# A hybrid decoder block on one core: the last sixteen tiles made of high and low halves

## The chip, the cores and the metric

The kernel runs on one core of a Trainium2 chip, written engine by engine in Bass: TensorE (PE), VectorE (DVE), ScalarE (ACT), GpSimd (POOL) and the sync engine (SP) each have their own list of instructions, and semaphores order them. The metric is the device time of one execution in microseconds, the median of several runs.

## The reference, cut to what matters

One decoder block on 272 tokens (16 meta tokens and 256) of width 1024, all in float32. The steps that the change touches are these:

```python
u = rms_norm(h, norm1_w)
proj = einsum('bld,dn->bln', u, w_in)          # 9232 columns: q,k,v | q,k,v | gate | beta, decay | gA | gB
y_a = differential_attention(...)              # 8 heads of 128
y_d = gated_deltanet(...)                      # chunked delta rule, 8 heads of 128
y_a = einsum('ble,ed->bld', y_a, w_branch_attn)
y_d = einsum('ble,ed->bld', y_d, w_branch_dn)
mixed = sigmoid(gate_a) * y_a + sigmoid(gate_d) * y_d
h = h + einsum('bld,de->ble', mixed, w_out)
h = h + hierarchical_moe(rms_norm(h, norm2_w), ...)   # 32 experts of width 256, top 2 in one of 4 groups
return rms_norm(h, final_norm_w)[:, 16:]
```

## The kernel before, in words

The products with `w_in`, `w_branch_attn`, `w_branch_dn` and `w_out` are cut into 96 tiles (`TILES`), eight of each kind, in the order ak, av, aq, dq, dk, dv, gate, ga, ya, gb, yd, out. Two tiles share a unit of 1 MB of weights; the sync engine loads units into a ring of six slots (L458), and slots 6 to 11 of the same ring hold buffers until the experts' weights come. A tile of ak to yd is the product of 128 weight columns with all tokens, 8 steps deep; TensorE's `tile(n)` writes it to bank n % 2.

Most tiles are made of halves: `split_high` (ScalarE, L278) rounds the 128x1024 weights of a tile to float32r (`w_hi`), `split_low` (VectorE, L283) subtracts that from the weights (`w_lo`), and TensorE takes hi x hi, hi x lo and lo x hi (L740), 24 matmuls of the program a tile. `SPLIT` lists these tiles, all but ya and out; `AHEAD = 3` says how many tiles ahead a split is made, and `NSPLIT = AHEAD + 2` how many pairs of buffers there are, in slots 6 to 10. The other operand is split once: `uT_hi`/`uT_lo` for the tokens, `yd_hi`/`yd_lo` for the delta rule's result. The ya tiles (L722, operand `yaT`) and the out tiles (L729, operands `mixT` and the ring's unit) are plain float32 products, 8 matmuls of the program each.

The order is written out by hand. Tiles up to dq go one after another. Then come 26 turns (`SLOTS_A`), in each of which TensorE does one tile (dq0 to gate1) and a part of the attention and of the convolution's sums, and VectorE one part of softmax, of the convolution (L1578) and of the gating (L1591), then the split (`split_lows`). The delta rule follows (`MIX_ORDER` for TensorE, `BEHIND` for the others): ten steps for the meta tokens, then 18 steps (s0 to s7, x1, t1, x2, t2, x3, t3, w, v, o, q) for each half of the tokens, each in two chains of four heads, with a tile between steps: ya0 before t3, ya1 before v, ya2 before o, ya3 after q of the first half and before s0 of the second, ya4 before s2, ya5 before s3, ya6 before s5, ya7 before s6. In `BEHIND` a split stands where its tile stands in `MIX_ORDER`, and the tile's evacuation (`tile_out`) behind the next step. GpSimd does one product in s1, s7, t1 and q (L651, L657).

Then gb4 to gb7, yd0 to yd7 and out0 to out7 run on TensorE back to back. For yd VectorE multiplies with the gate (L1652) and adds both branches into `mixT` (L1653, semaphore `mixed`); out0 waits for all of them. An out tile is one of the two halves of the tokens by 256 columns; VectorE adds it to `h_tok` (L1658). From out2 on TensorE turns the finished columns (`piece_turn`, L1003), and `piece_logits` (L1012) makes the router's logits of them; its first call waits for six small loads (`norms_in`) that ScalarE issues behind its last split (L1384 to L1389). The routing and eight batches of four experts end the kernel: gather (L1057), gate and up (L1069), down (L1088), back (L1095). The sync engine prefetches expert units as slots come free (`wait_tiles`), then 12 units for each batch, released by `gu_used` and `down_used`.

## Time and profile before

| | us |
|---|---|
| median of 3 runs | 745.88 (745.85 to 747.65) |
| the profiled execution | 743.06 |
| its span | 741.3 |
| TensorE busy | 628.2 (85%) |
| weight loads busy | 498.3 (67%) |
| VectorE busy | 322.0 (43%) |
| ScalarE busy | 247.1 (33%) |
| GpSimd busy | 46.1 (6%) |

The page cuts the span into 40 slices of 18.5 us; each digit is a busy share in tenths, PEclk the granted clock of TensorE in tenths of full speed:

```profile
PE   2899999899999979999898999976896686867954
DVE  4534349899878647522634273143210110201103
ACT  5335547667674434313222550121110110101102
PEclk9989999999999989999999999997999988978988
GB/s 292 252 137 167 157 153 114 105 70 112 114 114 132 153 57 59 59 57 57 52 132 104 2 260 262 423 255 1 346 422 422 422 422 422 422 422 423 421 385 57
```

Counted from 1, slices 7 to 13 are the attention turns, 14 to 23 the delta rule, 24 to 27 yd and out, and the experts begin in slice 28. Busy times are those of engines, which work beside each other, so they don't add up to the span; a busy share says nothing of what ends last.

### The profile page before, as it was taken

To read this page: it belongs to the slowest core of one execution; us is meant where nothing else is said; L and a number is where in the kernel's file an instruction comes from. 1 tells how busy PE (TensorE), PEld (TensorE's weight loads), DVE (VectorE), ACT (ScalarE), POOL (GpSimd) and SP (SyncE) were. 2 spreads that over 40 slices of the span, in tenths; PEclk is the share of its full clock that TensorE was granted. 3 is DMA by queue.
4 is the path that set the end of the run, shared out by engine and by line. 5 is a ranking of instruction groups with operands and counts; after the bars stand their busy time and mean duration, and the time that the engine had idled before them with its cause. 6 is when DMAs were issued, how large, how long until landed. Compare 5 with 4: busy or idle time off the path is not lost.

```text
span 741.3 us, 12849 instructions
## 1 busy us (share of the span) xinstructions
PE 628.2 (85%) x5127; PEld 498.3 (67%) x5127; DVE 322.0 (43%) x717; ACT 247.1 (33%) x548; POOL 46.1 (6%) x94
## 2 busy tenths in 40 slices
PE   2899999899999979999898999976896686867954
PEld 2899998789988879987788898854333323413321
DVE  4534349899878647522634273143210110201103
ACT  5335547667674434313222550121110110101102
POOL 8000000000000001201111100020000000000000
PEclk9989999999999989999999999997999988978988
DMA  9845443323334411111143077960899999999991
GB/s 292 252 137 167 157 153 114 105 70 112 114 114 132 153 57 59 59 57 57 52 132 104 2 260 262 423 255 1 346 422 422 422 422 422 422 422 423 421 385 57
DMA packets 69686, 156.40 MB, mean 211 GB/s; under 512 B 7042, under 2 KB 56308, under 8 KB 57348
## 3 DMA queue, kind: packets, MB, share of 16 engines
q1 hardware_dynamic: 65792, 154.36, 55.5%
q10 hardware_dynamic: 3844, 1.34, 0.7%
q8 instruction: 35, 0.57, 0.3%
q14 instruction: 15, 0.12, 0.0%
HBM read 154.64 MB, written 1.05 MB: 210 GB/s over the span
## 4 chain that ended last, share of the span: by engine, by line
PE 67%; DMA 16%; DVE 7%; ACT 4%; issue 3%; SPq 1%; POOL 1%; DVEq 0%; ACTq 0%; POOLq 0%
PE bank L740 29%; DMA arena<-in_expert_w_up_dram 15%; PE bank L1069 9%; PE bank L909 4%; PE bank L722 4%; PE bank L729 4%; PE bank L887 2%; PE bank L851 1%; PE bank L828 1%; PE bank L1088 1%; PE bank L1057 1%; SPq L481 1%; PE bank L1095 1%; PE bank L796 1%; DVE w_lo L283 1%
## 5 line engine op out<-in xcount | busy, mean ns | idle before, releaser
L740 PE MATMUL bank<-uT_hi,w_hi 128*128 128x272 f32 (+1 forms) x576 | 175.7, 305 | 5.7 <-issue 4.2
L740 PE MATMUL bank<-uT_lo,w_hi 128*128 128x272 f32 (+1 forms) x576 | 166.7, 289 | 0.0
L740 PE MATMUL bank<-uT_hi,w_lo 128*128 128x272 f32 (+1 forms) x576 | 166.5, 289 | 0.0
L283 DVE TENSOR_TENSOR w_lo<-arena,w_hi 128x1024 fp32r<-128x1024 f32 x80 | 98.6, 1235 | 48.3 <-ACT w_hi L278 48.0
L740 PEld LDWEIGHTS bank<-uT_hi,w_hi 128*128 128x128 f32 x576 | 111.4, 193 | 8.5 <-issue 6.8
L740 PEld LDWEIGHTS bank<-uT_lo,w_hi 128*128 128x128 f32 x576 | 111.5, 194 | 1.5 <-issue 0.5
L740 PEld LDWEIGHTS bank<-uT_hi,w_lo 128*128 128x128 f32 x576 | 111.3, 193 | 0.0
L1069 PE MATMUL bank<-arena 128*32 128x512 f32 x512 | 68.8, 698 | 42.3 <-DMA arena<-in_expert_w_up_dram 39.1
L278 ACT ACTIVATE w_hi<-arena 128x1024 fp32r<-128x1024 f32 x80 | 83.8, 1052 | 4.5 <-PE bank L740 4.2
L1069 PEld LDWEIGHTS bank<-arena 128*32 128x32 f32 x512 | 19.7, 126 | 85.7 <-issue 85.7
L1875 DVE COPY arena<-bank 128x256 f32<-128x256 f32 x8 | 3.4, 425 | 108.6 <-PE bank L1076 108.6
L1423 ACT ACTIVATE arena<-bank 128x256 f32<-128x256 f32 x8 | 3.1, 384 | 120.9 <-PE bank L1069 120.9
L1578 DVE SCALAR_TENSOR_TENSOR arena<-arena 128x272 f32<-128x272 f32 x72 | 37.8, 525 | 7.5 <-ACT arena L1210 5.8
L1088 PE MATMUL bank<-arena 128*32 128x512 f32 x256 | 34.0, 679 | 4.1 <-DVE arena L1882 4.1
L909 PE MATMUL bank<-arena 64*64 64x64 f32 x964 | 34.2, 220 | 1.5 <-ACT arena L1346 0.8
L909 PEld LDWEIGHTS bank<-arena 64*64 64x64 f32 x964 | 31.1, 134 | 5.8 <-issue 1.5
L1057 PEld LDWEIGHTS bank<-arena 128*128 128x128 f32 x256 | 31.1, 199 | 3.3 <-issue 3.3
L1057 PE MATMUL bank<-arena 128*128 128x128 f32 x256 | 31.2, 282 | 0.0
L1095 PE MATMUL bank<-arena 128*128 128x512 f32 x64 | 29.6, 605 | 0.0
L729 PE MATMUL bank<-arena 128*128 128x256 f32 x128 | 28.7, 380 | 1.1 <-DVE arena L1653 1.1
L722 PE MATMUL bank<-arena 128*128 128x256 f32 x128 | 29.3, 382 | 0.0
L729 PEld LDWEIGHTS bank<-arena 128*128 128x128 f32 x128 | 24.0, 190 | 4.3 <-issue 1.2
(319 smaller groups left out, 867.6 us busy)
## 6 DMA issues: line engine op xcount, KB each, us to landing
arena<-in_w_in_dram SPq DMA_DIRECT2D x36, 1024.0 KB, 5.2
arena<-in_expert_w_gate_dram SPq DMA_DIRECT2D x32, 1024.0 KB, 16.7
arena<-in_expert_w_up_dram SPq DMA_DIRECT2D x32, 1024.0 KB, 18.5
arena<-in_expert_w_down_dram SPq DMA_DIRECT2D x32, 1024.0 KB, 17.6
arena<-in_w_branch_attn_dram SPq DMA_DIRECT2D x4, 1024.0 KB, 5.0
arena<-in_w_branch_dn_dram SPq DMA_DIRECT2D x4, 1024.0 KB, 5.2
arena<-in_w_out_dram SPq DMA_DIRECT2D x4, 1024.0 KB, 5.1
arena<-in_x_dram SPq DMA_DIRECT2D x4, 512.0 KB, 5.0
```

What stands on the lines that cost most here:

```text
L278: nc.scalar.activation(w_hi[q % NSPLIT], split_source(nc.scalar, q), ACT.Copy).then_inc(w_hi_ready, 1)
L283: nc.vector.tensor_tensor(w_lo[q % NSPLIT], src, w_hi[q % NSPLIT].bitcast(F32), ALU.subtract).then_inc(w_lo_ready, 1)
L722: last = pe.matmul(ps[:, 0:SEQ], unit(u)[:, c, half * P:(half + 1) * P], yaT[:, c, :], start=(c == 0), stop=(c == NC - 1))
L729: last = pe.matmul(ps[:, 0:SEQ], mixT[:, c, t * P:(t + 1) * P], unit(u)[:, c, :], start=(c == 0), stop=(c == NC - 1))
L740: last = pe.matmul(ps[:, 0:b.shape[2]], a[:, c, :], b[:, c, :], start=(c == 0 and i == 0), stop=(c == NC - 1 and i == 2))
L887: last = pe.matmul(o[:, h, :], lhsT(h), rhs(h), start=start, stop=stop)
L909: last = pe.matmul(o[rows, h, :], lhsT[rows, h, :], rhs[rows, h, :], start=True, stop=True, tile_position=(q * Q, q * Q))
L1057: last = pe.matmul(bank[6 + group][:, (c % 4) * P:(c % 4 + 1) * P], u2[:, t, c * P:(c + 1) * P], pick[:, t].rearrange("p e s -> p (e s)"), ...
L1069: last = pe.matmul(bank[4][CAP * e:CAP * (e + 1), :], xg[:, c, CAP * e:CAP * (e + 1)], gate_up(e, odd)[:, c], start=(c == 0), stop=(c == N ...
L1088: last = pe.matmul(bank[6 + half][CAP * e:CAP * (e + 1), :], hidT[:, fc, CAP * e:CAP * (e + 1)], down_of(e)[:, fc, half * 512:(half + 1) * ...
L1095: last = pe.matmul(bank[2 * t + half][:, :], pickT[:, t, :], dsb[:, half * 512:(half + 1) * 512], start=False, stop=False, skip_group_chec ...
L1578: last = stt(a, x_[:, k:k + L], tap(k, c), a, ALU.mult, ALU.add)
```

## The change

`SPLIT` now holds the ya tiles too, and they are made like the others, with `ya_hi` and `ya_lo` as the second operand. These come from four copies on ScalarE and four subtractions on VectorE (`ya_split`), placed in `BEHIND` after steps s0 and s1 of the first half. The out tiles are made of three products as well: `mix_hi`/`mix_lo` by 128x256, `out_hi`/`out_lo` by 128x2048. `AHEAD` goes from 3 to 2, so there are four pairs of weight buffers in place of five; `ya_hi` lies where the fifth was. `out_hi` lies in slots 6 to 9, where the weight buffers were, and `out_lo` and `mix_lo` are written in place. Both engines do the mix halves between the splits of the yd tiles; ScalarE issues its six small loads after the last out half. The sync engine loads the experts' units of slots 6 to 9 with those of the out slots, behind the out tiles.

```diff
@@ -51,8 +51,8 @@
-SPLIT = [n for n, (kind, _) in enumerate(TILES) if kind not in ("ya", "out")]
-AHEAD = 3
+SPLIT = [n for n, (kind, _) in enumerate(TILES) if kind != "out"]
+AHEAD = 2
 NSPLIT = AHEAD + 2
@@ -102,7 +102,10 @@
         w_lo = [rounded(f"w_lo{i}", (TSLOTS + i) * UNIT + D, NC, P) for i in range(NSPLIT)]
-        spare = (TSLOTS + NSPLIT) * UNIT
+        ya_hi = rounded("ya_hi", (TSLOTS + NSPLIT) * UNIT, H, SEQ)
+        out_hi = [rounded(f"out_hi{i}", (TSLOTS + i) * UNIT, NC, 2 * P) for i in range(4)]
+        out_lo = [rounded(f"out_lo{i}", ((len(TILES) // 2 - 4 + i) % TSLOTS) * UNIT, NC, 2 * P) for i in range(4)]
+        spare = (TSLOTS + NSPLIT + 1) * UNIT
         gx, gs = at(spare, 2, SEQ), at(spare + 2 * SEQ, 2, SEQ)
@@ -134,6 +137,7 @@
         yaT_start = top[0]
+        ya_lo = rounded("ya_lo", yaT_start, H, SEQ)
         yaT = new(H, SEQ)
@@ -169,6 +173,7 @@
         new(H * SEQ)
+        mix_lo = rounded("mix_lo", top[0], NC, SEQ)
         gaT = new(H, SEQ)
@@ -191,6 +196,8 @@
         pick, pickw = new(TT, EPB, CAP), new(TT, EPB, CAP)
+        mix_hi = rounded("mix_hi", top[0], NC, SEQ)
         pickT = new(TT, P)
@@ -227,6 +234,8 @@
         yd_hi_ready, yd_lo_ready = sem("yd_hi_ready"), sem("yd_lo_ready")
+        ya_hi_ready, ya_lo_ready, mix_hi_ready, mix_lo_ready = sem("ya_hi_ready"), sem("ya_lo_ready"), sem("mix_hi_ready"), sem("mix_lo_ready")
+        out_hi_ready, out_lo_ready = sem("out_hi_ready"), sem("out_lo_ready")
         dn_pe = [sem("dn_pe_a"), sem("dn_pe_b")]
@@ -419,6 +428,7 @@
         held = []
+        steps_seen = 0
         for what in MIX_ORDER:
@@ -429,6 +439,10 @@
                 held = []
+
+                if len(META_STEPS) < steps_seen <= len(META_STEPS) + 4:
+                    BEHIND.append(("ya_split", steps_seen - len(META_STEPS) - 1))
+                steps_seen += 1
         BEHIND += held
@@ -485,7 +499,7 @@
-                    sp.wait_ge(tile_ready, FIRST["out"])
+                    sp.wait_ge(tile_ready, FIRST["out"] + (2 * (s - TSLOTS + 1) if s < TSLOTS + 4 else 0))
                 elif n in SPLIT:
@@ -495,16 +509,17 @@
             for s in range(SLOTS):
-                if s not in out_slots:
+                if s not in out_slots and not TSLOTS <= s < TSLOTS + 4:
                     wait_tiles(s)
...
                 load_unit(EPB, True, s)
-            for s in out_slots:
+            for i, s in enumerate(out_slots):
                 wait_tiles(s)
                 load_unit(0, False, s)
+                load_unit(0, False, TSLOTS + i)
             sp.wait_ge(tile_ready, len(TILES))
@@ -715,24 +730,24 @@
                 ps = bank[n % 2]
-                if kind == "ya":
-                    if j == 0:
-                        pe.wait_ge(qk_ready, NSS)
+                if kind == "out":
+
+                    t, i = j % 2, j // 2
+                    pe.wait_ge(mix_lo_ready, NC)
+                    pe.wait_ge(out_lo_ready, i + 1)
                     for c in range(NC):
-                        last = pe.matmul(ps[:, 0:SEQ], unit(u)[:, c, half * P:(half + 1) * P], yaT[:, c, :],
-                                         start=(c == 0), stop=(c == NC - 1))
-                elif kind == "out":
-
-                    t = j % 2
-                    pe.wait_ge(mixed, 2 * NC)
-                    for c in range(NC):
-                        last = pe.matmul(ps[:, 0:SEQ], mixT[:, c, t * P:(t + 1) * P], unit(u)[:, c, :],
-                                         start=(c == 0), stop=(c == NC - 1))
+                        for k, (a, b) in enumerate(((mix_hi, out_hi), (mix_hi, out_lo), (mix_lo, out_hi))):
+                            last = pe.matmul(ps[:, 0:SEQ], a[:, c, t * P:(t + 1) * P], b[i][:, c, :],
+                                             start=(c == 0 and k == 0), stop=(c == NC - 1 and k == 2))
                 else:
...
                         s_hi, s_lo = yd_hi, yd_lo
+                    elif kind == "ya":
+                        pe.wait_ge(ya_hi_ready, 4)
+                        pe.wait_ge(ya_lo_ready, 4)
+                        s_hi, s_lo = ya_hi, ya_lo
                     else:
@@ -1367,6 +1382,10 @@
                     pass
+                elif what == "ya_split":
+                    heads = slice(2 * arg, 2 * arg + 2)
+                    act.wait_ge(qk_ready, N_DN + 2 * arg + 2)
+                    act.activation(ya_hi[:, heads, :], yaT[:, heads, :], ACT.Copy).then_inc(ya_hi_ready, 1)
                 elif what == "result":
@@ -1378,9 +1397,26 @@
-            for n in range(FIRST["yd"], len(TILES)):
-                for q in splits_at(n):
+            def mix_high(j):
+                act.wait_ge(mixed, NC + j + 1)
+                act.activation(mix_hi[:, j, :], mixT[:, j, :], ACT.Copy).then_inc(mix_hi_ready, 1)
+
+            def out_high(i):
+
+                u = FIRST["out"] // 2 + i
+                act.wait_ge(slot_in[u % TSLOTS], 16 * (u // TSLOTS + 1))
+                act.wait_ge(tile_ready, FIRST["yd"] + 4 + i + 1)
+                act.activation(out_hi[i], unit(u), ACT.Copy).then_inc(out_hi_ready, 1)
+
+            for j in range(NC):
+                for q in splits_at(FIRST["yd"] + j):
                     split_high(q)
+                if j:
+                    mix_high(j - 1)
+                if j >= 5:
+                    out_high(j - 5)
+            mix_high(NC - 1)
+            out_high(3)
             act.dma_start(norm2_b, row(norm2_w, D)).then_inc(norms_in, 16)
@@ -1774,6 +1810,10 @@
                     scale_by(SPREAD[arg])
+                elif what == "ya_split":
+                    heads = slice(2 * arg, 2 * arg + 2)
+                    dve.wait_ge(ya_hi_ready, arg + 1)
+                    tt(ya_lo[:, heads, :], yaT[:, heads, :], ya_hi[:, heads, :].bitcast(F32), ALU.subtract).then_inc(ya_lo_ready, 1)
                 elif what == "result":
@@ -1788,8 +1828,25 @@
-            for n in range(FIRST["yd"], len(TILES)):
-                split_lows(n)
+            def mix_low(j):
+                dve.wait_ge(mix_hi_ready, j + 1)
+                tt(mix_lo[:, j, :], mixT[:, j, :], mix_hi[:, j, :].bitcast(F32), ALU.subtract).then_inc(mix_lo_ready, 1)
+
+            def out_low(i):
+                dve.wait_ge(out_hi_ready, i + 1)
+                tt(out_lo[i], unit(FIRST["out"] // 2 + i), out_hi[i].bitcast(F32), ALU.subtract).then_inc(out_lo_ready, 1)
+
+            for j in range(NC):
+                split_lows(FIRST["yd"] + j)
+                tile_out(FIRST["yd"] + j)
+                if j:
+                    mix_low(j - 1)
+                if j == 6:
+                    out_low(0)
+            mix_low(NC - 1)
+            for n in range(FIRST["out"], len(TILES)):
+                if n < FIRST["out"] + 3:
+                    out_low(n - FIRST["out"] + 1)
                 tile_out(n)
```

## Rows read from the trace of the kernel before

**Rows 1.** Stretches: busy of PE, PEld, DVE, ACT, POOL; PEclk, DMA share, GB/s
```profile
317.00:384.00 67.00, 60.52 (x610) 53.31 (x609) 25.05 (x55) 15.10 (x32) 5.08 (x4) 1.00 0.18 58
...
540.00:600.00 60.00, 43.69 (x295) 18.73 (x288) 7.74 (x20) 5.73 (x8) 0.00 (x0) 0.89 1.01 422
```

**Rows 2.** The chain that ended last: start us, us, what
```profile
457.65 10.60 PE bank L729 x48
...
513.44 7.07 PE bank L1069 x64
...
545.97 18.34 DMA arena<-in_expert_w_up_dram
```

**Rows 3.** Timeline of the sync queue, 434 to 530 us: start, us, what
```profile
490.93 0.43 SPq L481 DMA_DIRECT2D arena<-in_expert_w_up_dram  x1
520.74 0.35 SPq L481 DMA_DIRECT2D arena<-in_expert_w_gate_dram  x1
```

**Rows 4.** The chain again: a ya tile, then gb0
```profile
325.30 3.46 PE bank L722 x16
...
384.34 2.84 PE bank L740 x24
```

**Rows 5.** Timeline around the end of ya3: GpSimd and TensorE
```profile
345.46 2.50 POOL L657 TENSOR_TENSOR gateT<-gateT,arena 128x512 f32<-128x512 f32 x2 [35.84 <-DVE arena L1766]
...
346.87 3.81 PE L887 MATMUL bank<-arena 128*128 128x128 f32 x32
```

**Rows 6.** VectorE's splits: the page's group, then one of 128x512 in the timeline
```profile
L283 DVE TENSOR_TENSOR w_lo<-arena,w_hi 128x1024 fp32r<-128x1024 f32 x80 | 98.6, 1235 | 48.3 <-ACT w_hi L278 48.0
...
430.01 0.68 DVE L1781 TENSOR_TENSOR yd_lo<-gateT,yd_hi 128x512 fp32r<-128x512 f32 x1
```

**Rows 7.** Timeline of s1 to s3 of the first half: VectorE twice, TensorE
```profile
277.33 0.69 DVE L1711 TENSOR_TENSOR arena<-bank,arena 128x512 f32<-128x512 f32 x1 [1.78 <-PE bank L887]
...
284.12 1.22 DVE L283 TENSOR_TENSOR w_lo<-arena,w_hi 128x1024 fp32r<-128x1024 f32 x1
...
284.45 4.88 PE L909 MATMUL bank<-arena 64*64 64x64 f32 x160
```

**Rows 8.** Low halves and tile starts, steady (dk5), ramp (dq5); TensorE waits
```profile
169.24 1.22 DVE L283 TENSOR_TENSOR w_lo<-arena,w_hi 128x1024 fp32r<-128x1024 f32 x1
171.90 0.49 PE L740 MATMUL bank<-uT_hi,w_hi 128*128 128x272 f32 x1
...
126.21 1.22 DVE L283 TENSOR_TENSOR w_lo<-arena,w_hi 128x1024 fp32r<-128x1024 f32 x1
126.08 0.49 PE L740 MATMUL bank<-uT_hi,w_hi 128*128 128x272 f32 x1
...
PE bank L828 <- ACT arena L1272: 2.9, 2, 2.7
```

**Rows 9.** Timeline near dv6: the low half of dv7, and a wait of TensorE
```profile
211.39 1.22 DVE L283 TENSOR_TENSOR w_lo<-arena,w_hi 128x1024 fp32r<-128x1024 f32 x1
...
216.42 0.44 PE L754 MATMUL bank<-arena 128*128 128x128 f32 x2 [1.28 <-DVE arena L1591]
```

**Rows 10.** Timeline: VectorE takes yd7; a ScalarE pass of 128x256
```profile
456.62 0.42 DVE L1652 TENSOR_TENSOR arena<-bank,arena 128x256 f32<-128x256 f32 x1 [1.95 <-PE bank L740]
...
465.29 0.42 ACT L1399 ACTIVATE arena<-arena 128x256 f32<-128x256 f32 x1 [14.57 <-DVE arena L1658]
```

**Rows 11.** Small loads: last issue, router product, landings (last number)
```profile
448.94 0.46 ACTq L1389 DMA_DIRECT2D arena<-in_router_expert_b_dram  x1
...
472.14 0.98 PE bank L1012 x4
...
arena<-in_router_group_b_dram ACTq DMA_DIRECT2D x1, 2.0 KB, 7.4
...
arena<-in_w_in_dram ACTq DMA_DIRECT2D x1, 64.0 KB, 8.9
```

**Rows 12.** One stretch of line 740 on TensorE, columns as in rows 1
```profile
403.60:406.80 3.20, 3.20 (x17) 0.50 0.00 0
```

More of the change, by code:

```diff
@@ L193, in hybrid_block @@
         pick, pickw = new(TT, EPB, CAP), new(TT, EPB, CAP)
+        mix_hi = rounded("mix_hi", top[0], NC, SEQ)
+        assert top[0] >= zone + 2 * UNIT
         pickT = new(TT, P)
```

## The prediction

> **What bounds the kernel now.** I read the profile in four steps. First the stretches: which engine is full where, and at which granted clock [rows 1]. From 317 to 384 us TensorE is busy 60.5 of 67 us while VectorE is busy 25 and the DMA engines are nearly idle; from 540 us on the DMA engines are full at 422 GB/s and TensorE has air. Second the chain that ended last [rows 2]: up to 520.5 us it runs almost wholly through TensorE's tiles, with short pieces of VectorE and ScalarE between, and from batch 2 of the experts on it alternates between one DMA wait of some 18 us and one gate/up product. Third the sync engine's queue [rows 3]: the last prefetch of expert weights is issued at 490.93, then nothing until 520.74, right behind batch 0's gate/up product, and from there the stream never pauses. So the time is what TensorE needs to reach the end of batch 0's gate/up, plus a fixed stream of bytes. A microsecond won on TensorE's path before 520 us is a microsecond of the total, as long as the prefetch ends before that product. Fourth, the waits inside the delta rule (260 to 430 us), where TensorE, VectorE and ScalarE hand over to each other and the new splits land.
>
> **The tiles themselves: 9.9 us.** A tile in plain float32 ("ya", "out") is 16 matmul instructions in the trace and takes 3.46 us from its start to the next work; a tile of the same 128x128 by 128x256 shape in high and low halves (gb0) is 24 instructions and takes 2.84 us at the same full granted clock [rows 4]. The moving side of an out tile keeps 256 contiguous columns, so 2.84 is the price there too. 3.46 - 2.84 = 0.62 us a tile; 8 ya tiles give 4.96, 8 out tiles 4.96, together 9.92 us, if what stands behind a tile wasn't waiting for something else anyway.
>
> The Trainium skill ("FP8 and Floating Point Precision", TensorE Precision Notes) says that true FP32 is four passes through the array. Three single-pass products would by that be three quarters of 3.46, 2.60 us, and the sum 16 x 0.86 = 13.8 us instead of 9.9. The row has this kernel's split tile at 2.84, and the sum goes by it.
>
> **Who stands behind each ya tile: -0.5 us.** After ya0, ya1, ya2, ya4, ya5, ya6 and ya7 the delta rule's operands are ready before a tile 0.62 us shorter would end. After ya3, which ends where the next product starts at 346.87, comes step s0 of the second half, and that needs the gate product of GpSimd: two of them in 2.50 us from 345.46 on [rows 5], so the first ends at about 346.7. s0 can't start before 346.8, and of ya3's 0.62 only 0.1 is left (bounds 0.4 and 0.6).
>
> **Splits of the ya weights: 0, up to 1.0.** Each ya tile now brings one ScalarE copy and one VectorE subtraction (1.22 us, the mean of the page 1.235 [rows 6]) into the delta rule. VectorE has 42 idle us of 67 there [rows 1]. Only before s2 and s3 of the second half does it stand close, and there the same sequence of the first half has its split at 284.12 and still lets TensorE run s3 and s4 through, 160 instructions in 4.88 us from 284.45 on [rows 7]. With that cover gone the two would cost one subtraction less 0.2 of slack: 1.0.
>
> **Halves of the attention's result: -0.4 us.** Four copies and four subtractions of 128x512 (0.68, some 0.6 from start to start [rows 6]) are put between s0 and s2 of the first half, where the path is VectorE's. The first one delays s1 of one chain, which GpSimd then finishes inside the ga1 tile; the second falls into VectorE's idle 1.78 us before 277.33; the third and fourth delay s2, behind which VectorE takes its next work at 284.12 and s3 starts at 284.45, 0.3 later [rows 7]. Two times 0.6 exposed is the upper bound 1.2, all of it hidden the lower bound 0. I take 0.4.
>
> **Two tiles ahead instead of three: -0.2 us.** The low half of a tile is now made one VectorE turn later, when the next one's was made. In the steady attention turns that is still in time: the turn's subtraction at 169.24 ends 1.4 us before the tile that would now need it starts at 171.90 [rows 8]. In the ramp it is late: dq5 started at 126.08 and would wait for the subtraction of 126.21, which ends at 127.43, 1.35 later [rows 8]; dq4 comes 1.2 and dq3 1.0 late in the same way. But there VectorE sets the pace and doesn't wait for these tiles, and TensorE then waits 2.7 us for it and for ScalarE's square ahead of dq6 [rows 8]. That wait swallows the delay. Near dv6 the half would end at 212.6 and TensorE started it at 211.9, 0.7 late; the path runs through ScalarE there, and TensorE waits 1.28 us for VectorE at 216.42 [rows 9]. The upper bound is both delays in full, 1.35 + 0.72 = 2.1; the lower is 0. I take 0.2.
>
> **Handing over from yd to out: -1.0 us.** The last yd product is taken at 456.62, the mix sum follows and TensorE starts at 457.65 [rows 2, 10]. Now a ScalarE copy and a VectorE subtraction of 128x256 stand between: 0.42 each in like rows [rows 10], and two handovers of about 0.1. The other mix halves and out_low(0) are made during yd tiles, each with 1.95 us of waiting on VectorE [rows 10]; out_low(1) to (3), 1.22 each, lie inside out tiles, where VectorE has one sum of 0.42 a tile. The first out tile starts 1.0 later (bounds 0.8 and 1.4).
>
> **The router's weights: -0.4 us, up to 3.0.** ScalarE issues six small DMAs; the last one at 448.94 [rows 11], 6.4 after the first. They now stand behind mix_high(7) and out_high(3), which begins at about 458.0, and behind them wait the table load and the squares. In the frame of the old trace the fifth is issued at 461.3 and the sixth at 464.4. The fifth took 7.4 us to land [rows 11]: 468.7, and the sixth is not much later. The router's first product waits for all six. It stood at 472.14 [rows 11] and now comes at 458.65 + 3 x 2.84 + 0.43 (the turn) + 2.84 = 470.4, 1.7 behind that landing. Under a filled sync queue a small load of this queue took 8.9 us near the start of the kernel [rows 11]; for the sixth that is 473.4, 3.0 late. The near row was taken at 325 to 400 GB/s, so I go by it, with 0.4 for the sixth.
>
> The Trainium skill ("DMA: Bandwidth & Descriptors", Queues, rings and completion order) has each DMA engine take turns between queues packet by packet; by that the expert units that sync has issued just before don't hold the small loads back, this term is 0 and the sum 7.8. The 8.9 us above speak against relying on it.
>
> **The sync queue: 0.** Eight expert units were issued at out's start or before; now slots 6 to 9 go with the out slots, two after each second tile. Four units are issued when the last out tile ends, where it was three: 10 us of transfer at 422 GB/s. The first reader is gate/up at 513.44 [rows 2], 23 us after that tile. GpSimd gets nothing new.
>
> **Sum.** 9.92 - 0.5 - 0.4 - 0.2 - 1.0 - 0.4 = 7.4 us. The profiled execution took 743.06 us (span 741.3 and 1.8 around it), 2.8 under the median 745.88; the differences are microseconds of its own trace, so the forecast is 735.7 for such an execution and 738.5 for a median.
>
> **Rivals.**
> (a) The router's weights come late: 3.0 instead of 0.4, 741.1. For it: a full DMA queue. Against: a landing at a like rate. 14%.
> (b) The shorter lead is not absorbed: 2.1 instead of 0.2, 740.4. For it: the late halves. Against: TensorE's own wait behind them. 9%.
> (c) Slower: VectorE becomes the bound of the delta rule. Its additions are 8 x 1.22 + 4 x 0.6 = 12.2 us; exposed in full they turn the -8.9 of tiles and handover into +3.3, 749.2. It is slower once more than 8.9 of the 12.2 us are exposed. Against: 42 idle us of 67. 5%.
> (d) The expert stream takes the gain back, because the prefetch ends late: no change, 745.9. Against: 23 us of room. 4%.
> (e) The change does not do what it says, the products keep float32's pace: the handover alone, 746.9. Against: gb0 does it. 3%.
>
> **How the numbers follow.** The forecast has 60%; 5% stay for what I don't see. TensorE falls to half of its clock in single stretches, as for 3.2 us near 403.6 with 17 products at work in it [rows 12], which take 2.84 / 24 = 0.118 each at the full one; one stretch more or fewer is some 1.3 us. Low end: the open terms at 0 (8.4) and one stretch fewer, 9.8: 736.1; I take 735.5. High end: (a) and one stretch more: 742.5; I take 743.0. A measurement of this kernel tells about 0.3%, 2.2 us. Faster 0.88, from the forecast, (a), (b) and the unseen; same 0.05, (d) and part of (e); slower 0.07, (c) and the rest of (e).
>
> **What would show it.** Right: 24 instructions in 2.84 us in every ya and out tile; the first out product about 2 us after the last yd product is taken; batch 0's gate/up ending near 513; the stream from there to the end as long as before. Wrong: TensorE idle before the router's product, released by the scalar queue's DMAs (a); the start of dq7 later than before (b); waits on VectorE between 265 and 385 us (c); the stream's restart not right behind gate/up (d).

## The result

The changed kernel takes 751.5 us, the median of 6 runs (750.62 to 755.58); the kernel before, measured beside it, took 744.68 (6 runs, 740.12 to 747.65). The ratio is 1.010, 95% interval 1.006 to 1.014: slower by 1%, where 738.5 and faster had been forecast. The profiled execution of the changed kernel took 755.58 us (span 753.8), the slowest of its six, and the profiled one of before 743.06 (span 741.3). So 12.5 us lie between the two traces and 6.8 between the medians; the other 5.7 us of what the traces show belong to the two executions and not to the kernels, and a section below says in which stretches single executions differ.

The chain of waits of the changed kernel, around the place where the time comes in (start us, us, what):

```profile
452.18 2.20 DVE out_lo L1837
454.38 0.34 DVE arena L1688
...
456.76 7.52 ACTq L1423
464.31 13.30 ACTq L1424
477.64 4.00 DMA arena<-in_router_expert_b_dram
481.68 1.92 PE bank L1027 x4
483.60 1.15 PE bank L1033 x2
484.75 3.82 PE bank L740 x24
489.01 2.83 PE bank L740 x24
...
516.48 5.83 PE bank L1072 x32
523.91 7.07 PE bank L1084 x64
```

Up to 452 us the chain is TensorE's tiles as before. From 456.8 to 481.6 it leaves TensorE and runs through ScalarE's DMA queue: the issue of two small loads, of 7.52 and 13.30 us, and the landing (the time from issue until the data are there) of a third. The router's first product, at 472.14 in the trace of before [rows 11], starts at 481.68. Batch 0's gate/up product (now line 1084) starts at 523.91 against 513.44 [rows 2]. The tiles themselves do what was forecast: where the full clock is granted, an out tile is 24 instructions in 2.83 us, as in this chain, and a ya tile 24 in 2.85.

Waits between 440 and 500 us, changed kernel (engine, line <- released by: us in total, times, longest):

```profile
ACT L1431 <- issue: 20.7, 1, 20.7
...
PE bank L1027 <- DMA arena<-in_router_expert_b_dram: 11.9, 1, 11.9
...
PE bank L740 <- DVE mix_lo L1833: 2.6, 1, 2.6
```

In the trace of before neither of the last two is there; the first was 5.9 us, hidden. The issues of expert units on the sync queue, and the first and the sixth of the small loads on ScalarE's (the fourth and the fifth are the 7.52 and 13.30 us in the chain), timeline of the changed kernel:

```profile
453.79 0.80 SPq L495 DMA_DIRECT2D arena<-in_expert_w_down_dram  x2
455.20 0.33 SPq L495 DMA_DIRECT2D arena<-in_expert_w_gate_dram  x1
455.57 0.45 SPq L495 DMA_DIRECT2D arena<-in_expert_w_up_dram  x1
463.69 0.80 SPq L495 DMA_DIRECT2D arena<-in_expert_w_gate_dram  x2
469.77 0.81 SPq L495 DMA_DIRECT2D arena<-in_expert_w_up_dram  x2
...
455.29 0.35 ACTq L1420 DMA_DIRECT2D arena<-in_norm_w_dram  x1
...
477.64 0.46 ACTq L1425 DMA_DIRECT2D arena<-in_router_expert_b_dram  x1
```

and the landings of two of them (last number, us):

```profile
arena<-in_router_expert_w_dram ACTq DMA_DIRECT2D x1, 128.0 KB, 23.6
arena<-in_router_group_w_dram ACTq DMA_DIRECT2D x1, 16.0 KB, 23.8
```

Four units of 1 MB are issued from 453.79 to 456.0, around the first of the small loads, and four more while the others wait. In the trace of before the same six went out from 442.50 to 448.94, with one unit just ahead and one beside them, and landed in 4.5 to 7.4 us (the 7.4 is in [rows 11]). Moving ScalarE's copies ahead of these loads moved the loads 13 us, into the stretch in which the expert stream begins.

The packets of the two DMA queues say why the small loads came so late. Here are the packets, the MB and the busy share of each queue (q1 is the sync engine's, q10 ScalarE's), for 468 to 472 us of the changed kernel and then for 472 to 484 us of b_late, a run described below:

```profile
q1 hardware_dynamic: 229, 1.62, 98.9%
q10 hardware_dynamic: 229, 0.01, 3.4%
...
q1 hardware_dynamic: 673, 4.98, 99.7%
q10 hardware_dynamic: 673, 0.01, 3.3%
```

The queues take turns, one packet each. The sync queue's packets are of some 7 KB on average, those of ScalarE's queue of 16 bytes: the 16-KB load of the group router's weights is written into rows of four columns and so is cut into 1024 pieces of 16 bytes, and the 128-KB load into 1024 of 128 bytes. Some 57 pieces a microsecond get through beside the sync queue; in a_gate (below), where nothing else is in flight, ScalarE's queue moved 2337 packets in the 4 us from 456 to 460. In the changed kernel not one of the 128-byte pieces moved before 478 us, when the eight expert units were almost through, and the last ones moved at 481: the small loads in fact landed behind the bulk.

From 540 us on the stream is as before, 422 GB/s as in [rows 1]; the stretches of the changed kernel that answer to [rows 1], same columns:

```profile
317.00:384.00 67.00, 60.38 (x714) 56.72 (x712) 37.32 (x63) 23.57 (x42) 7.38 (x6) 0.95 0.22 74
...
456.00:482.00 26.00, 13.73 (x101) 13.43 (x102) 9.06 (x9) 4.52 (x10) 0.00 (x0) 0.76 0.93 360
...
540.00:600.00 60.00, 47.66 (x319) 23.13 (x317) 9.10 (x24) 6.32 (x9) 0.00 (x0) 0.91 1.01 422
```

VectorE's load between 317 and 384 us rose from 25.05 to 37.32 busy us (forecast were 12.2 more) and still leaves 30 idle. The line of 456 to 482 us is the wait: TensorE is busy half of it, while the DMA engines are at 0.93.

### The profile page after: what moved, and what is told of

It reads as the page before. It is cut to its first block, busy times and chain, and to the rows that moved or that the text cites. A ratio compares the mean times of both kernels' runs of the same rounds, so it can differ in the third digit from the quotient of the medians.

```text
span 753.8 us, 13198 instructions
## 1 busy us (share of the span) xinstructions
PE 626.8 (83%) x5255; PEld 500.7 (66%) x5255; DVE 347.2 (46%) x741; ACT 267.3 (35%) x572; POOL 45.6 (6%) x94
## 3 DMA queue, kind: packets, MB, share of 16 engines
HBM read 154.64 MB, written 1.05 MB: 207 GB/s over the span
## 4 chain that ended last, share of the span: by engine, by line
PE 54%; DMA 16%; DVE 14%; issue 5%; ACT 5%; ACTq 3%; SPq 1%; POOL 0%; DVEq 0%; POOLq 0%
PE bank L755 26%; DMA arena<-in_expert_w_up_dram 15%; PE bank L1084 9%; PE bank L924 4%; DVE w_lo L292 3%; DVE arena L1614 2%; ACTq L1424 2%; PE bank L740 2%; PE bank L866 1%; PE bank L1103 1%; PE bank L902 1%; DVE arena L1653 1%; PE bank L1072 1%; ACTq L1423 1%; SPq L495 1%
## 5 line engine op out<-in xcount | busy, mean ns | idle before, releaser
L292 DVE TENSOR_TENSOR w_lo<-arena,w_hi 128x1024 fp32r<-128x1024 f32 x88 | 111.3, 1265 | 59.2 <-ACT w_hi L287 58.8
L1084 PE MATMUL bank<-arena 128*32 128x512 f32 x512 | 69.6, 705 | 41.8 <-DMA arena<-in_expert_w_up_dram 38.6
L287 ACT ACTIVATE w_hi<-arena 128x1024 fp32r<-128x1024 f32 x88 | 92.3, 1051 | 0.3 <-issue 0.3
L1084 PEld LDWEIGHTS bank<-arena 128*32 128x32 f32 x512 | 20.1, 128 | 85.7 <-issue 85.7
L1103 PE MATMUL bank<-arena 128*32 128x512 f32 x256 | 35.7, 708 | 4.1 <-DVE arena L1939 4.1
L1072 PEld LDWEIGHTS bank<-arena 128*128 128x128 f32 x256 | 32.0, 204 | 3.3 <-issue 3.3
L1930 DVE COPY arena<-bank 128x512 f32<-128x512 f32 x8 | 5.5, 692 | 43.7 <-PE bank L1072 43.7
L1103 PEld LDWEIGHTS bank<-arena 128*32 128x32 f32 x256 | 8.6, 126 | 25.5 <-issue 19.8
L1110 PEld LDWEIGHTS bank<-arena 128*128 128x128 f32 x64 | 11.5, 189 | 18.2 <-issue 18.2
```

The source lines that it names most:

```text
L287: nc.scalar.activation(w_hi[q % NSPLIT], split_source(nc.scalar, q), ACT.Copy).then_inc(w_hi_ready, 1)
L292: nc.vector.tensor_tensor(w_lo[q % NSPLIT], src, w_hi[q % NSPLIT].bitcast(F32), ALU.subtract).then_inc(w_lo_ready, 1)
L1072: last = pe.matmul(bank[6 + group][:, (c % 4) * P:(c % 4 + 1) * P], u2[:, t, c * P:(c + 1) * P], pick[:, t].rearrange("p e s -> p (e s)"), ...
L1084: last = pe.matmul(bank[4][CAP * e:CAP * (e + 1), :], xg[:, c, CAP * e:CAP * (e + 1)], gate_up(e, odd)[:, c], start=(c == 0), stop=(c == N ...
L1103: last = pe.matmul(bank[6 + half][CAP * e:CAP * (e + 1), :], hidT[:, fc, CAP * e:CAP * (e + 1)], down_of(e)[:, fc, half * 512:(half + 1) * ...
L1110: last = pe.matmul(bank[2 * t + half][:, :], pickT[:, t, :], dsb[:, half * 512:(half + 1) * 512], start=False, stop=False, skip_group_chec ...
```

## The experiments

All ratios are against the kernel before, run beside each kernel on the same chip, with the 95% interval. There were three such groups, on three chips: a_sp, a_gate, b_late and b_ya (before: 745.88 us); b_sp, b_ahead2, b_out_sp and a_order (743.74); a_halves and a_halves_gate (745.74). Across groups only the ratios are to be compared, not the medians. Two numbers from each trace are used throughout: where the yd7 tile starts, and how long it is from there to the gather product of batch 0 (line 1057 of before), the first work of the experts on TensorE. In the trace of before these are 453.58 us and 53.4 us; in the changed kernel's 450.75 and 65.7. So the changed kernel's trace arrives 2.8 us earlier at yd7 and loses 12.3 between there and the experts. Of the 2.8, 1.0 was there at the tile ak4, ahead of anything that the change touches.

| kernel | ratio | median, us | yd7 starts | yd7 to gather | gather to end |
|---|---|---|---|---|---|
| before | | 745.88 | 453.58 | 53.4 | 234.3 |
| changed | 1.010 (1.006 to 1.014) | 751.5 | 450.75 | 65.7 | 237.3 |
| a_sp | 0.990 (0.9855 to 0.9945) | 739.98 | 450.94 | 51.4 | 238.1 |
| a_gate | 0.9922 (0.9894 to 0.9951) | 739.52 | 449.40 | 51.4 | 238.0 |
| b_late | 1.0229 (1.0183 to 1.0274) | 762.75 | 453.71 | 72.0 | 235.9 |
| b_sp | 1.0036 (1.0009 to 1.0063) | 746.68 | 454.07 | 53.4 | 238.2 |
| b_ahead2 | 0.9995 (0.9966 to 1.0025) | 744.44 | 453.31 | 53.4 | 238.3 |
| b_ya | 0.9917 (0.9888 to 0.9945) | 737.84 | 448.07 | 53.4 | 234.3 |
| b_out_sp | 0.9975 (0.9954 to 0.9996) | 742.12 | 450.37 | 49.9 | 238.1 |
| a_order | 0.9907 (0.9877 to 0.9937) | 737.6 | 451.22 | 49.6 | 235.2 |
| a_halves | 0.9885 (0.984 to 0.993) | 735.84 | 449.68 | 47.1 | 237.9 |
| a_halves_gate | 0.9862 (0.9816 to 0.9907) | 733.87 | 451.23 | 47.2 | 234.4 |

Theory A: the small loads are late because they run beside the expert units, and that alone makes the change slower. Its rival: the handover from yd to out, or the copies on ScalarE and VectorE, cost the time, and the late loads only fill a gap that would be there anyway.

### Take the small loads away from the expert units

**a_sp**: the changed kernel with the six loads issued by the sync engine, behind the loads of h_tok and ahead of the first expert unit.

```diff
                     for t in range(TT):
                         sp.dma_start(h_tok[:, t, :], x[0, t * P:(t + 1) * P, :]).then_inc(h_in, 16)
+                    sp.dma_start(norm2_b, row(norm2_w, D)).then_inc(norms_in, 16)
...
+                    sp.dma_start(r_b[:, 4:36], row(router_expert_b, 32)).then_inc(norms_in, 16)
...
-            act.dma_start(norm2_b, row(norm2_w, D)).then_inc(norms_in, 16)
...
-            act.dma_start(r_b[:, 4:36], row(router_expert_b, 32)).then_inc(norms_in, 16)
```

> The changed kernel with one move: the six small loads for the router and the norms are issued by the sync queue, behind the two loads of the residual's tokens and ahead of the last unit of w_out, instead of by ScalarE behind the last out half. Theory A (the wait of TensorE for these loads, 11.9 us in the trace of the changed kernel, is the whole reason why it is not faster): the wait is gone, the ratio to the kernel before is 0.984 to 0.992, some 734 to 740 us beside 745. Rival B (the out stage is lost to other things, the handover and half clock, and the loads only hide that): under 5 us are won against the changed kernel, the ratio stays above 1.000.

Measured: 0.990, and the time from yd7 to the experts falls from 65.7 to 51.4 us. The issue of the 2-KB load still took 6.40 us, on the sync engine, but ahead of the expert stream nothing waited for it.

**a_gate** leaves the loads where the change puts them and holds the other side back: the sync queue waits for them ahead of its third expert unit.

```diff
                 if s not in out_slots and not TSLOTS <= s < TSLOTS + 4:
                     wait_tiles(s)
+                    if s == TSLOTS + 4:
+                        sp.wait_ge(norms_in, 16 * 6)
```

> The changed kernel with one wait added on the sync queue: the units of slots 10 and 11 and all behind them are loaded only when the six small loads have landed. ScalarE issues these where the change put them, at about 455 us. Theory A (the expert units in flight hold them back): the issues take 7 us in place of 22.8, they land by 467, TensorE waits at most 1 us for them, and as the prefetch still ends before batch 0 the ratio to the kernel before is 0.984 to 0.994. Rival B (the small loads are slow by themselves, or through their own queue): the issues take over 15 us whatever the sync queue does, and the later prefetch makes it slower than 751.

Measured: 0.9922. Same place and almost the same moment as in the changed kernel, no expert unit behind the second in flight, timeline and landings of a_gate:

```profile
455.29 0.61 ACTq L1425 DMA_DIRECT2D arena<-in_router_expert_w_dram  x1
455.93 3.02 ACTq L1426 DMA_DIRECT2D arena<-in_router_group_b_dram  x1
...
arena<-in_router_expert_w_dram ACTq DMA_DIRECT2D x1, 128.0 KB, 4.8
```

The 128-KB load's issue takes 0.61 us instead of 7.52, the next 3.02 instead of 13.30, and the landing 4.8 instead of 23.6. TensorE doesn't wait for them.

**b_late** does the reverse to the kernel before: nothing of the change, only the six loads held until the mix is done.

```diff
+            act.wait_ge(mixed, 2 * NC)
             act.dma_start(norm2_b, row(norm2_w, D)).then_inc(norms_in, 16)
```

> The kernel before with one wait added: ScalarE issues the same six small loads only after the last sum of both branches, some 15 us later than before, when the sync queue has issued its expert units. Everything else is as before. Theory A (small loads behind a filled sync queue take over 20 us from the first issue to the last landing, instead of 11): TensorE waits 8 to 14 us ahead of the router's first product, 753 to 759 us beside 745. Rival B (the long issue belongs to the new placing of work on ScalarE or to the new units): they land before they are wanted, 745 to 748.

Measured: 1.0229, above the expected 753 to 759 us, with the changed kernel's pattern, only larger: TensorE waited 16.8 us and not 8 to 14. Here eight units went out on the sync queue from 456.74 to 460.9, and the first small load at 457.67 (timeline and waits of b_late):

```profile
459.44 7.15 ACTq L1388 DMA_DIRECT2D arena<-in_router_expert_w_dram  x1
466.62 17.80 ACTq L1389 DMA_DIRECT2D arena<-in_router_group_b_dram  x1
...
PE bank L1012 <- DMA arena<-in_router_expert_b_dram: 16.8, 1, 16.8
```

Taking the overlap away in two different ways makes the change faster than before, putting it into the old kernel makes that slower by 17 us. Theory A is shown, and its rival is left with what the handover costs, some 3 us (below). Between the two ways of taking it away no difference was measured.

### The parts of the change one by one

**b_sp**: the kernel before, only the loads moved as in a_sp. It tells how much of a_sp is the move itself.

> The kernel before, with only the six small loads for the norms and the router moved from ScalarE's queue to the sync queue, behind the loads of h_tok. In the kernel before PE waits nowhere for the router's weights, so by the theory that their place matters only when they come late, the ratio is 0.997 to 1.003. The rival: ScalarE's issues of 7 us each between the mixed and the output tiles cost time in the kernel before too, and the move gains 2 to 4 us by itself, ratio 0.995 to 0.997; then that gain is no part of what the changed kernel's tiles bring.

Measured: 1.0036 (1.0009 to 1.0063), just above the expected 1.003. The move gains nothing, so the rival is refuted; if anything it costs. Its time from yd7 to the experts is the old 53.4 us.

**b_ahead2**: the kernel before with the shorter lead alone.

```diff
-AHEAD = 3
+AHEAD = 2
```

> The kernel before with AHEAD = 2 and nothing else of the change: the halves of a tile's weights are made two tiles ahead instead of three. Forecast's step (0.2 us, up to 0.7 us for late halves at dv6 and dv7): 745.9 + 0.2 = 746.1, ratio 0.998 to 1.002. Rival (the price of each late start of the delta rule's tiles stays, 2.1 us): ratio 1.003. If it is below 0.996, half of the gain of the run with the attention branch's part alone (ratio 0.9917, which has the same shorter lead) is the lead's and not the tiles'.

Measured: 0.9995 (0.9966 to 1.0025), and the trace shows more than that. Tile dq2 starts 0.95 us ahead of the trace of before, dq5 0.50 behind it (so the three late halves cost 1.45 there), dq7 2.81 ahead, gate0 1.86 ahead. Two stretches, of before and then of b_ahead2 (columns as in [rows 1]):

```profile
126.00:134.00 8.00, 5.33 (x39) 4.53 (x39) 7.68 (x22) 3.79 (x13) 0.42 (x1) 1.00 0.17 50
134.00:142.00 8.00, 8.00 (x49) 7.29 (x48) 6.50 (x21) 5.82 (x18) 0.73 (x2) 0.79 0.38 129
```

```profile
126.00:134.00 8.00, 6.95 (x49) 5.84 (x48) 7.65 (x26) 4.43 (x15) 0.68 (x2) 1.00 0.43 133
134.00:142.00 8.00, 8.00 (x63) 7.19 (x61) 7.72 (x20) 5.58 (x17) 0.48 (x2) 1.00 0.42 131
```

In the trace of before TensorE idled 2.67 us in one piece near 131 to 134 and then ran part of the next stretch at the lower of its levels (granted clock 0.79 over the stretch); with the late halves the idle time is cut into pieces, the one left is 1.05 us, and the clock stays at 1.00. That is no accident of one execution: the wait ahead of dq6 is 2.7 us and the granted clock from 134 to 142 us 0.78 or 0.79 in each of the three traces with the longer lead (before, b_late, b_sp), and 1.0 to 1.1 us and 1.00 in all nine with the shorter lead. From dq2 to gate0 these nine gain 0.85 to 0.93 us on the trace of before.

**b_ya**: the kernel before with the shorter lead and the attention branch's part only; the out tiles stay plain float32.

```diff
-SPLIT = [n for n, (kind, _) in enumerate(TILES) if kind not in ("ya", "out")]
+SPLIT = [n for n, (kind, _) in enumerate(TILES) if kind != "out"]
```

> The kernel before with the attention branch's part of the change alone: ya tiles in three products, their splits and those of the result, two tiles ahead instead of three; the out tiles are plain float32 and the small loads where they were. By the trace of the changed kernel up to yd (0.6 us a ya tile less, 1.5 lost behind ya3, the shorter lead absorbed): 3 to 4 us faster, ratio 0.994 to 0.997. Rival B (the delta rule takes it all back on VectorE): 0.999 or more.

Measured: 0.9917, a larger gain than the expected 0.994 to 0.997. From yd7 on its trace is that of before (53.4 and 234.3 us); all of its gain stands ahead of yd7, 5.5 us in this trace. Not all of that is the change: 1.4 us were there at ak4, and 1.5 came in the tile gb3, whose 24 products took 3.04 us here and 4.55 in before, at another granted clock.

**b_out_sp**: the output's part, the shorter lead and the small loads on the sync queue, without the attention branch's part.

> The output's part of the change alone, with the shorter lead and with the six small loads issued on the sync queue; the attention branch's tiles stay single products of unsplit operands. Forecast's sum for the output: 8 tiles x 0.62 = 4.96 us gained, less the handover. The handover measured in the changed kernel was 2.6 us behind the last yd tile (1.07 before) plus a first tile of 4.5 us at the half clock against 3.46, so 4.96 - 1.5 - 1.0 = 2.4 us: ratio 0.995 to 0.998 against before. Rival (the output's part is worth nothing, since the expert weights stream sets when the experts begin): ratio 0.999 to 1.002.

Measured: 0.9975, and against b_sp, which has the loads in the same place, 0.9975 / 1.0036 = 0.994, or 4.5 us. From yd7 to the experts it is 49.9 us against 53.4. The ya part, b_ya over b_ahead2, is 0.9917 / 0.9995 = 0.992, or 5.8 us. These two ratios and the 1.0036 multiply to 0.990 for a_sp, which measured 0.990: the parts add up, within intervals of 0.003 each.

### The handover

The changed kernel's first out tile waits 2.6 us for mix_lo, 1.5 more than out0 of before. A part of it is out_low(0): it takes 2.28 us on VectorE, not 1.22, because out_hi and out_lo are 128 x 2048, and it stood ahead of the mix of yd7. By the chain above VectorE takes yd7 at 454.38, 3.6 us after that tile's start; in before [rows 10] it was 3.0, and in a_order, which has out_low(0) out of the way, it is 3.0 again. So some 0.5 us of the 1.5 are out_low(0)'s; the other 1.0 is the copy and the subtraction of the last mix half, as forecast. The group of the four out_low in the changed kernel:

```profile
L1837 DVE TENSOR_TENSOR out_lo<-arena,out_hi x4: 2281/2283/2286, 452.1 to 464.0; 128x2048 fp32r<-128x2048 f32 x4
```

(durations in ns, smallest, median, largest.) **a_order** is a_sp with out_low(0) moved behind the last mix_low and the first out tile taken by term, low halves last.

```diff
+                    if j == 0:
+                        order = [(c, k) for k in range(3) for c in range(NC)]
...
-                if j == 6:
-                    out_low(0)
             mix_low(NC - 1)
+            out_low(0)
```

> The changed kernel with the six small loads on the sync queue, and with the first output tile taken apart by term: eight products of high halves, each waiting for its own mix_hi piece, then eight with mix_lo, then eight with out_lo(0), whose subtraction is moved from ahead of the last two yd tiles' halves to behind mix_low(7). Nothing is left out. If the handover (2.6 us of idle PE, and half clock behind it) costs what its rows say, this is 1.5 to 3 us below the same kernel with the handover as it was (ratio 0.990): 0.986 to 0.989. Rival (VectorE's 2.28 us for out_lo(0) then ends last, behind the yd tiles, and PE waits for that instead): the same as with the old handover, 0.990, and the wait of 2.3 us shows ahead of the first tile's last eight products.

Measured: 0.9907, the same as a_sp within the intervals and as its rival had it, not the expected 0.986 to 0.989; the traces differ, 49.6 against 51.4 us from yd7 to the experts. The rival's wait is there too (timeline of a_order, TensorE):

```profile
454.06 0.99 PE L759 MATMUL bank<-out_hi,mix_hi 128*128 128x256 f32 x7
455.65 0.38 PE L759 MATMUL bank<-out_hi,mix_hi 128*128 128x256 f32 x1 [0.60 <-ACT mix_hi L1421]
...
458.31 1.22 PE L759 MATMUL bank<-out_lo,mix_hi 128*128 128x256 f32 x8 [1.34 <-DVE out_lo L1850]
```

**a_halves** puts out_low(0) in two halves into two gaps of 1.62 us that the trace of a_order shows on VectorE, and lets the first out tile wait for mix_lo piece by piece. **a_halves_gate** is the same on a_gate.

```diff
+                if j in (5, 6):
+                    part = slice((j - 5) * NC // 2, (j - 4) * NC // 2)
+                    last = tt(out_lo[0][:, part, :], unit(FIRST["out"] // 2)[:, part, :],
+                              out_hi[0][:, part, :].bitcast(F32), ALU.subtract)
...
-                    pe.wait_ge(mix_lo_ready, NC)
                     pe.wait_ge(out_lo_ready, i + 1)
                     for c in range(NC):
+                        if j == 0:
+                            pe.wait_ge(mix_lo_ready, c + 1)
```

> The changed kernel with the six small loads on the sync queue, and the handover to the output's tiles mended without changing the order of the products: out_low(0) (2.28 us) is done in two halves, one in each of VectorE's 1.62-us gaps behind mix_low(4) and mix_low(5), and the first output tile waits for each mix_lo piece at its own step of the contraction instead of for all eight. From the last yd tile to the first down product of the experts the kernel before took 53.4 us, the same kernel with the loads alone moved 51.4, the one with the first tile taken by terms 49.6. If the two waits that were left there (0.60 and 1.34 us) go, that stretch is 47.9 to 48.9 and the ratio 0.984 to 0.990. Rival (PE is held up by the first half's subtraction in the yd tiles, or by mix_lo(7)): 49.5 or more, ratio 0.990.

> The same handover, but the six small loads stay on ScalarE's queue, and the sync queue holds the experts' units from the ninth on until those loads have landed. Theory: what counts is only that the small loads don't run beside the experts' units, so this is the same as with the loads on the sync queue, within 0.3%: ratio 0.984 to 0.990, stretch 47.9 to 48.9 us. Rival: the gap that the gate leaves in the stream of units (the queue stood from 453.8 to 462.4 us in the kernel with the old handover) makes the first experts late once the output is faster: VectorE or PE then waits for a unit before the first expert, and the ratio is 0.3% or more higher than with the sync queue.

Measured: 0.9885 and 0.9862. No wait is left between the yd and the out tiles, and the first three out tiles run at a granted clock of 1.00; the chain of a_halves_gate:

```profile
454.24 8.54 PE bank L743 x72
```

against 10.60 for the same three tiles of before [rows 2] and 10.16 in a_gate, where the granted clock behind the wait was 0.73 from 455 to 461 us. Yd7 to the experts is 47.1 and 47.2 us: 6.3 less than before, where the eight tiles explain 5.0 and the old wait of 1.07 that is gone the rest. That is better than the 47.9 to 48.9 expected: the expectation had subtracted the two waits, 1.94 us, from a_order's 49.6. But a_order's first out tile takes 5.31 us from its start at 454.06 to the next one's at 459.37, 2.48 more than 2.83, so each break in it cost some 0.3 us more than the idle time in its row. The gap that the gate leaves in the stream costs nothing. These two have the lowest ratios here, both inside what was expected and under 1 with their whole interval.

## Why the prediction was wrong

**The router's weights: this is the step that failed.** The place was right, and it was rival (a); the size was not. The sum had 0.4 us and the upper bound 3.0. TensorE waited 11.9 us, and with the granted clock of 0.65 from 481.6 to 489 us, behind that wait (the router's product 1.92 instead of 0.98, the next 1.15 instead of 0.63, out4 3.82 instead of 2.83) it comes to 14.3 us, the difference between 65.7 and a_gate's 51.4. Two errors make it up. The forecast set the issues of the fifth and the sixth load at 461.3 and 464.4, taking the issue times of the trace of before for durations of these instructions:

```profile
444.05 1.66 ACTq L1387 DMA_DIRECT2D arena<-in_router_expert_w_dram  x1
445.74 3.18 ACTq L1388 DMA_DIRECT2D arena<-in_router_group_b_dram  x1
```

The issues were longer with more in flight: 7.52 and 13.30 us in the changed kernel. And it bounded the landing by 8.9 us, the worst small load of that queue in [rows 11], though no row showed one beside eight units of 1 MB. It named "a filled sync queue" and then took the near row instead. A bound from a row with another load on the DMA engines is no bound. With 14.3 in the place of 0.4, the forecast 738.5 becomes 752.4; measured were 751.5. That the two are so near is in part luck, since the 14.3 is read from single traces and the errors below stand beside it.

The Trainium skill ("DMA: Bandwidth & Descriptors", Queues, rings and completion order) has each engine take turns between queues packet by packet. The trace agrees on the turns: 229 packets of each queue in the same 4 us. What failed is what the prediction drew from it, that the expert units then don't hold the small loads back and the term is 0. A turn is one packet, however small: the 1024 packets of 16 bytes each let a packet of some 7 KB go first, and the 1024 of 128 bytes stood behind them. Beside the expert units the 16-KB load took 23.8 us to land, without them 4.7 (a_gate).

**Handing over to out: mis-sized.** Forecast 1.0 (0.8 to 1.4), with 1.22 us for each out_low, the mean of 128x1024; the tiles are 128x2048 and take 2.28. The step also said that out_low(0) lies in a wait of VectorE of 1.95 us, which 2.28 doesn't fit. TensorE's wait was 2.6 against 1.07 before, 1.5 more: the forecast 1.0 and the 0.5 of out_low(0). Behind it the first tiles ran in part at the half clock: 10.16 us in a_gate for what took 8.54 in a_halves_gate, 1.6 more. Together 3.1: a_gate gains 2.0 us between yd7 and the experts, where eight tiles alone would gain 5.0. b_out_sp has the same wait of 2.6 us and a clock of 1.00 behind it, and gains 3.5: the wait is there in all four traces with this handover, the half clock behind it in three of them, and what decides that was not found.

**The tiles: right.** 2.83 to 2.86 us a tile at the full clock, against 3.46. b_ya and b_out_sp show the two halves of the sum in the time: 5.8 and 4.5 us, against a forecast of 4.96 - 0.5 - 0.4 and 4.96 - 1.0. The second fits, the first is better than forecast by some 1.7; that is inside the intervals, and the traces don't bear it out: from ga0 to yd7, with the clock of gb3 taken out, the seven with split ya tiles are 2.7 to 3.7 us shorter than b_ahead2.

**The shorter lead: the late halves right, their effect not.** The late halves at dq3 to dq5 and dv6 came as worked out (1.45 and 0.69 us), the wait ahead of dq6 swallowed the first as forecast. The net gain of 0.9 us, with the higher granted clock behind that wait, was not foreseen. In the time it is nothing.

**Behind ya3: right in the mechanism, 0.9 us for 0.5.** TensorE waits 0.55 us for GpSimd there in the changed kernel. The start of ya4 loses 2.1 of what was won, but 1.2 of that is the clock: b_ahead2 and b_sp, which have no split ya tile, lose it in the same place, 352 to 358 us, when they arrive early (granted clock 0.50 and 0.54 there, 1.00 in before). Lines of before, then b_ahead2:

```profile
357.26 0.63 PE L919 MATMUL bank<-arena 128*128 128x128 f32 x4 [2.71 <-issue]
357.72 1.06 PE L887 MATMUL bank<-arena 128*128 128x128 f32 x8
```

```profile
355.42 1.09 PE L919 MATMUL bank<-arena 128*128 128x128 f32 x4 [2.01 <-issue]
356.30 1.92 PE L887 MATMUL bank<-arena 128*128 128x128 f32 x8
```

**Halves of the attention's result: within the bounds.** From ga0 to ya0 three of the seven traces that have them lose nothing and four lose 0.7 us; 0.4 was taken, with bounds of 0 and 1.2.

**The sync queue and rivals (c), (d), (e).** VectorE did not become the bound: it kept 30 idle us of 67 beside the ya tiles. The stream restarts right behind gate/up, at 531.21 against a product that ends at 530.98, as it should. (e) is refuted by every out tile.

**The range.** It held the known terms at their rows and gave the router's weights 3.0 us of room and 14% as a rival; nothing beyond was priced. The miss is that tail: the other errors are 2.1 us at the handover, 1.7 the other way in the ya part and 1.1 the other way in the lead (0.9 gained where 0.2 was charged).

## What is not the change

A single trace has several microseconds of its own. By ak4, ahead of anything that the change touches, the eleven other traces stand from 0.1 us behind to 2.4 ahead of the trace of before. In one tile, gb3, the clock gives 3.04, 4.55 or 5.42 us for the same 24 products. From the gather to the end the traces take 234 to 236 us or 237 to 238, whether they have the change or not: the kernel before has 234.3, the same kernel with the shorter lead 238.3. The gather product shows it first, the last down products last (the chain, before and then b_ahead2):

```profile
506.98 4.87 PE bank L1057 x32
...
725.28 3.64 PE bank L1088 x32
```

```profile
506.73 6.33 PE bank L1057 x32
...
727.33 5.29 PE bank L1088 x32
```

Those two lines are 3.1 of the 4.0 us. What decides which of the two an execution takes was not found. But b_sp and b_ahead2, which have nothing of the change there, show the longer form too, so the 3.0 us by which the changed kernel's trace is longer behind the gather can't be put down to the change, and it is the reason why differences under 3 us between single traces were read by stretch here, and never from the total.

## What to carry to other kernels

Before moving small loads, or work ahead of them on the issuing engine, look at what the other queues have in flight at the new moment: a row for the same load beside a lighter queue is no bound. Count the pieces of the small load, not its bytes: beside the stream it got one piece through for each bulk packet. Loads that gate a later step are best issued before a bulk prefetch begins, or the prefetch is held until they have landed; either gave back 14 us here, and the hold cost nothing that could be measured. And read the shape of each new instruction in the diff before pricing it, since a helper named like another can work on twice the tile.

## What the runs showed of the hardware

- Two DMA queues with work take turns packet by packet, whatever the sizes: 229 packets each in 4 us and 673 each in 12 us, 16 bytes a packet on one side and some 7 KB on the other. The queue of small pieces moved 0.01 MB in those 12 us, the other one 4.98.
- The issue of a DMA can hold its engine for many microseconds: the issue of a 2-KB load took 3.02, 3.18, 6.40, 13.30 and 17.80 us in five kernels. In the changed kernel ScalarE stood idle for 20.7 us ahead of its table load. What ends such an issue was not found.
- Loads landed the later the smaller their pieces: beside the expert units the two 512-KB loads of the norms, in pieces of 4 KB, landed in 8.6 and 13.5 us, the 16-KB and the 128-KB one of the router behind them in 23.8 and 23.6, and 4.7 and 4.8 us without the units. The router's weights in larger pieces were not tried.
- Idle time cut into pieces went with a higher granted clock: with 1.45 us of late halves spread over three tiles, one wait of 2.67 us was 1.05, and the granted clock behind it 1.00 instead of 0.79, a gain of 0.9 us net in nine traces of nine.
